# A hybrid decoder layer on one core: the output projection by seven half products for eight in blocks 7 to 14

## What is computed

```python
h = rmsnorm(x, norm_g)
proj = h @ w_in
q_g, k_g, v_g, gk_lr, gate_g, u_p, gate_p, q_m, gate_m = jnp.split(proj, SPLIT_IDX, axis=-1)
...
gk = jax.nn.log_sigmoid(gk_logit) / GLA_NORMALIZER
o_gla = gla_chunked(...)                 # 4 heads, chunks of 64, a carried state
o_gla = (rmsnorm(o_gla, gla_norm_g).reshape(B, T, D_GLA) * silu(gate_g))
o_pool = (pooled @ pool_w * pool_scale * silu(gate_p))   # windows 2, 4, 8, 16
o_mem = (softmax(q_m k_m) v_m) * silu(gate_m)            # 256 memory rows
mixed = jnp.concatenate([o_gla, o_pool, o_mem], axis=-1)
x = x + mixed @ w_out
return rmsnorm(x, final_g)
```

## Time and profile before

| | |
|---|---|
| median of three runs | 1374.71 us (1374.44 to 1376.68) |
| the profiled execution | 1374.43 us, span 1372.7 us |
| PE, PEld busy | 98%, 74% |
| DVE, ACT, POOL busy | 62%, 57%, 27% |
| DMA | 269.33 MB, mean 196 GB/s |
| chain that ended last | PE 94%, DVE 3%, ACT 1%, DMA 1% |
| L682 (values and output projection), L721 (seven-product groups), L700 (whole groups) | 34%, 33%, 10% of the chain |

### The profile page before, as it was taken

The page is one execution under the profiler, slowest core; times in us unless marked ns, Lnnn a source line. Parts: engine busy times, 40 slices in busy tenths (PEclk is TensorE's granted clock), DMA queues, the critical chain, the costliest instruction groups (busy, mean ns, idle before and its releaser), DMA issues.

```text
span 1372.7 us, 35629 instructions
## 1 busy us (share of the span) xinstructions
PE 1348.0 (98%) x14751; PEld 1012.2 (74%) x14751; DVE 844.3 (62%) x1598; ACT 783.9 (57%) x1446; POOL 371.6 (27%) x313
## 2 busy tenths in 40 slices
PE   6999999999999999999999999999999999999997
PEld 5788668586695968769586785958779596876953
DVE  6876667576555565565665655566565556566455
ACT  7896645555545565564646546464664556556353
POOL 2120163135322142332223223222332214233100
PEclk9999999999999999999999999999999999999999
DMA  9576657663663737466374754637466373745641
GB/s 385 192 214 210 215 181 236 194 245 121 215 247 94 285 100 264 182 184 245 94 293 124 242 205 149 251 96 278 150 215 247 111 270 98 264 181 183 241 101 47
DMA packets 143768, 269.33 MB, mean 196 GB/s; under 512 B 75152, under 2 KB 88720, under 8 KB 140432
## 3 DMA queue, kind: packets, MB, share of 16 engines
q1 hardware_dynamic: 142912, 266.20, 56.8%
q10 hardware_dynamic: 720, 1.06, 0.2%
HBM read 220.03 MB, written 30.41 MB: 182 GB/s over the span
## 4 chain that ended last, share of the span: by engine, by line
PE 94%; DVE 3%; ACT 1%; DMA 1%; issue 1%; SPq 0%; ACTq 0%; DVEq 0%
PE bank L682 34%; PE bank L721 33%; PE bank L700 10%; PE bank L916 2%; PE bank L942 2%; PE bank L936 2%; PE bank L1002 2%; PE bank L927 1%; PE bank L1032 1%; PE bank L957 1%; PE bank L803 1%; PE bank L900 1%; DVE arena L1638 1%; DMA out_parts<-fg 1%; PE bank L787 1%
## 5 line engine op out<-in xcount | busy, mean ns | idle before, releaser
L682 PE MATMUL bank<-ring,arena 128*128 128x512 f16 x1440 | 318.6, 379 | 0.0
L682 PEld LDWEIGHTS bank<-ring,arena 128*128 128x128 f16 x1440 | 138.5, 98 | 165.3 <-issue 5.9
L721 PE MATMUL bank<-arena,ring 128*128 128x128 f16 x4032 | 237.1, 219 | 0.0
L721 PE MATMUL bank<-arena,wres 128*128 128x128 f16 x4032 | 237.0, 219 | 0.0
L721 PEld LDWEIGHTS bank<-arena,ring 128*128 128x128 f16 x4032 | 228.4, 98 | 5.2 <-DVE arena L1616 1.8
L721 PEld LDWEIGHTS bank<-arena,wres 128*128 128x128 f16 x4032 | 227.7, 98 | 2.5 <-issue 2.5
L682 PE MATMUL bank<-wv,arena 128*128 128x512 f16 x768 | 168.5, 379 | 0.2 <-DVE wv L1602 0.2
L2136 POOL TENSOR_TENSOR arena<-arena 128x1024 f32<-128x1024 f32 (+2 forms) x42 | 64.8, 1543 | 352.9 <-ACT arena L1082 350.7
L682 PEld LDWEIGHTS bank<-wv,arena 128*128 128x128 f16 x768 | 75.0, 98 | 87.8 <-DVE wv L1602 0.4
L2144 POOL TENSOR_TENSOR arena<-arena 128x1024 f16<-128x1024 f32 x32 | 67.5, 2130 | 194.9 <-ACT arena L1100 182.3
L700 PE MATMUL bank<-arena,wres 128*128 128x256 f16 x768 | 86.1, 273 | 0.4 <-DVE wres L1580 0.4
(11 more groups left out here) (268 smaller groups left out, 2085.2 us busy)
## 6 DMA issues: line engine op xcount, KB each, us to landing
ring<-out_parts SPq DMA_DIRECT2D x120, 512.0 KB, 5.4
ring<-gate_parts SPq DMA_DIRECT2D x92, 512.0 KB, 5.8
ring<-side_parts SPq DMA_DIRECT2D x92, 512.0 KB, 6.3
arena<-in_xt SPq DMA_DIRECT2D x16, 1024.0 KB, 6.0
arena<-in_x SPq DMA_DIRECT2D x32, 512.0 KB, 4.4
out<-arena SPq DMA_DIRECT2D x31, 512.0 KB, 2.9
arena<-in_w_out SPq DMA_DIRECT2D x16, 512.0 KB, 5.3
out_parts<-arena SPq DMA_DIRECT2D x6, 512.0 KB, 6.4
```

What stands on the lines that cost most here:

```text
L682: mm = nc.tensor.matmul(ap, lhs, rhs, start=k == 0 and n == 0, stop=(k, n) == last)
L721: mm = nc.tensor.matmul(ap, w[:, p, k, j * P:(j + 1) * P], x_part(r, b)[:, k, :], start=fresh and j == 0 and k == 0 and n == 0, stop=k == ...
```

## The change

- **Products.** In steps 7 to 14 (of blocks 6 to 13's rows) the output product is a 2x2 block product over rows, features and columns with seven half products of 12 matmuls (`out_seven`). They stand where the quarters stood: 0 and 1 for quarter 0, 2 and 3 for 1, 4 and 5 for 2, and 6 alone for 3. They go to banks 0, 1, 0, 1, 6, 0, 1; products 2 and 5 add onto what stands in bank 0. Products 0 to 3 and 6 use rows of `mixed` (in the second half of the rows the two feature halves have been summed in place), product 2 the sum S2, products 4 and 5 a second set of sums written over the first rows of `mhl`.
- **Sums of mixed rows** (`mixed_sums`, POOL): three tensor_tensor, of 512, 512 and 1024 elements, at the start of step i, once the maximum of mixed is known; the third writes into `yb`'s place and waits for its store. ACT and DVE split them (`split_hi`, `split_lo`, two each per block).
- **Additions.** `add_seven` on DVE, nine of 512 elements in place of four. The first 128 rows of y have a place of their own (`y0`).
- **Sums of W_out.** In blocks 3 to 6 a pair of tiles of W_out is loaded per block (`pair_in`), scaled (`pair_scaled`, ACT), summed (`out_sums`, four tensor_tensor of 512 elements on POOL), split (`sums_hi`, `sums_lo`) and stored to DRAM (`sums_out`, 1 MB). ACT's x_plain moves behind norm_y there, and behind p_hi(3) in steps 7 to 14.
- **Loads.** 14 slots of 512 KB per block for the output product in place of 8; those for products 4, 5 and 6 are issued between the turns (the DMA transposes of the memory probabilities), before the loads of the next block's gates.
- **Blocks 4 to 6** are written out; the loop is over 7 to 14.

```diff
@@ -86,6 +86,11 @@
...
+OUT_BANK = (0, 1, 0, 1, 6, 0, 1)
+OUT_SLOT = ((7, 2), (3, 4), (5, 6), (0, 1), (2, 7), (3, 4), (5, 6))
+OUT_SPLIT = (1, 1, 2, 1, 3, 3, 1)
...
@@ -199,6 +229,10 @@
...
+        y0 = view(O_TP + 4096, [D], F32)
+        s43 = view(O_Y, [KT, P], F32)
+        wpair = [view(O_TP + 4096 * n, [2, 512], F32) for n in range(2)]
+        wsum = view(O_MIX, [4, 2, 512], F16)
...
@@ -372,7 +407,9 @@
...
-            with eng.Fori(WHOLE, NB - 1) as i:
+            for i in range(WHOLE, SEVEN):
+                step(i, False, False, False)
+            with eng.Fori(SEVEN, NB - 1) as i:
                 step(i, False, False, False)
...
@@ -431,6 +477,38 @@
...
+            def pair_in(i):
+                k = sum_row(i)
+                if is_whole(i):
+                    sp.wait_ge(lo_c, COMBINED + len(MADE))
+                else:
+                    sp.wait_ge(ad[PM], 4 * (i + 1))
+                    sp.wait_ge(q_ok, 2 * (i + 1))
+                    sp.wait_ge(qm_lo, 2 * (i + 1))
+                for n in range(2):
+                    sp.dma_start(wpair[n].rearrange("p h c -> p (h c)"), w_out[:, k + 4 * n, :]).then_inc(d_wot[n], 16)
+            def sums_out(i):
+                k = sum_row(i)
+                sp.wait_ge(lo_o, KT + 2 * k + 2)
+                sp.dma_start(sums_d[:, :, k // 2, :, k % 2, :], wsum).then_inc(d_wot[2], 16)
...
@@ -497,10 +575,23 @@
...
+            def residual_seven(i, t):
+                j = i - 1
...
+                else:
+                    sp.wait_ge(m_lo, mixed_split(i) + 3)
+                sp.dma_start((y0, yb)[t], x[j * TB + t * P:j * TB + (t + 1) * P, :]).then_inc(d_res, 16)
...
@@ -561,6 +652,50 @@
...
+                    to_slot(7, wo_d[:, 0, 0, :, :, :].rearrange("p r k c -> p (r k c)"))
+                    sums_in(3, T1)
+                    sp.wait_ge(pe_f[PM], 3 * i + 2)
+                    to_slot(2, wo_d[:, 0, 1, :, :, :].rearrange("p r k c -> p (r k c)"))
+                    quads_in(1, 0, 1)
+                    sp.wait_ge(pe_f[PM], 3 * i + 3)
+                    sum_in(2, T2, 0)
+                    residual_seven(i, 0)
+                    turn(i, 0)
+                    turn(i, 1)
+                    sp.wait_ge(pe_out, out_made(i) + 1)
+                    quads_in(4, 1, 1)
+                    sp.wait_ge(pe_out, out_made(i) + 2)
+                    sums_in(5, T3)
+                    residual_seven(i, 1)
+                    turn(i, 2)
+                    turn(i, 3)
+                    sp.wait_ge(pe_out, out_made(i) + 3)
+                    sums_in(6, T4)
+                    sp.wait_ge(pe_out, out_made(i) + 4)
+                    gates_in((0, 1))
+                    sp.wait_ge(pe_out, out_made(i) + 5)
+                    gates_in((2,))
+                    sides_in((0,))
+                    sp.wait_ge(pe_out, out_made(i) + 6)
+                    gates_in((3, 4))
+                    store(i - 1, 0)
+                    sp.wait_ge(pe_out, out_made(i) + 7)
+                    gates_in((5, 6))
+                    sp.wait_ge(d_store, 16 * (2 * i - 1))
...
@@ -575,22 +710,26 @@
...
+                    if makes_sums(i):
+                        pair_in(i)
                 for n in range(4):
                     turn(i, n)
+                if makes_sums(i):
+                    sums_out(i)
...
@@ -748,16 +887,38 @@
...
 
+            def out_seven(i, n):
+                pe.wait_ge(m_hi, mixed_split(i) + OUT_SPLIT[n])
+                pe.wait_ge(m_lo, mixed_split(i) + OUT_SPLIT[n])
+                if n in (2, 3, 5):
+                    pe.wait_ge(y_add, rows_added(i) + {2: 1, 3: 2, 5: 3}[n])
+                if n == 4:
+                    pe.wait_ge(sT_ok, 2 * i + 2)
+                if n == 6:
+                    pe.wait_ge(y_add, rows_added(i) + 8)
+                for s in OUT_SLOT[n]:
+                    pe.wait_ge(d_slot[s], 16 * loads("out" if n < 4 else "more", i, s))
+                first, t = 4 * (n in (1, 5, 6)), n in (3, 6)
+                for k in range(4):
+                    w = ring[:, OUT_SLOT[n][k // 2], :].rearrange("p (r k c) -> p r k c", r=2, k=2)
+                    for m, (p, r) in enumerate(((0, 0), (0, 1), (1, 0))):
+                        lhs = s2hl[:, p, k, :] if n == 2 else mhl[:, p, first + k, t * P:(t + 1) * P]
+                        mm = nc.tensor.matmul(bank[OUT_BANK[n]][:, :], lhs, w[:, r, k % 2, :],
+                                              start=n not in (2, 5) and k == 0 and m == 0, stop=k == 3 and m == 2,
+                                              skip_group_check=True)
+                mm.then_inc(pe_out, 1)
             def mix_sum(n):
 
...
@@ -953,12 +1114,17 @@
...
                 def quarter(n):
-                    if not first:
+                    if is_seven(i, last):
+                        for m in ((0, 1), (2, 3), (4, 5), (6,))[n]:
+                            out_seven(i, m)
...
@@ -1202,17 +1368,44 @@
...
+            def split_hi(i, n):
+                if n == 2:
+                    act.wait_ge(ms_ok, 3 * (i - SEVEN) + 2)
+                    nc.scalar.activation(s2hl[:, 0, :, :], sg[0], ACT.Copy, scale=s_m).then_inc(m_hi, 1)
+                else:
+                    act.wait_ge(ms_ok, 3 * (i - SEVEN) + 3)
+                    act.wait_ge(pe_out, out_made(i) + 2)
+                    nc.scalar.activation(mhl[:, 0, :, 0:P], s43, ACT.Copy, scale=s_m).then_inc(m_hi, 1)
...
@@ -1382,6 +1582,8 @@
...
+                    if is_seven(i, last):
+                        split_hi(i, 2)
...
@@ -1449,6 +1651,10 @@
...
+                elif makes_sums(i):
+                    pair_scaled(i)
+                elif is_seven(i, last):
+                    split_hi(i, 3)
...
@@ -1460,8 +1666,15 @@
...
-                if not first:
-                    norm_y(i - 1, 0)
+                if is_seven(i, last):
+                    x_plain(i + 1)
+                    norm_y(i - 1, 0, rows_added(i) + 5, y0)
+                elif not first:
+                    if makes_sums(i):
+                        sums_hi(i)
+                    norm_y(i - 1, 0, rows_added(i) + 2)
+                if makes_sums(i):
...
@@ -1695,9 +1908,23 @@
...
+            def sums_lo(i, n):
+                k = sum_row(i)
+                dve.wait_ge(hi_o, KT + 4 * k + 3 + n)
+                nc.vector.tensor_tensor(wsum[:, 2 * n:2 * n + 2, 1, :], wpair[n], wsum[:, 2 * n:2 * n + 2, 0, :],
+                                        ALU.subtract).then_inc(lo_o, 1)
+            def split_lo(i, n):
+                dve.wait_ge(m_hi, mixed_split(i) + n)
+                out2 = (s2hl[:, 0, :, :], s2hl[:, 1, :, :]) if n == 2 else (mhl[:, 0, :, 0:P], mhl[:, 1, :, 0:P])
+                nc.vector.scalar_tensor_tensor(out2[1], sg[0] if n == 2 else s43, s_m, out2[0], ALU.mult,
+                                               ALU.subtract).then_inc(m_lo, 1)
...
@@ -1707,18 +1934,33 @@
...
+            def add_seven(i, m):
+                t, h, b, made, before = (None, (0, 0, 0, 1, 0), (0, 0, 1, 2, 1), (0, 1, 0, 3, 0), (0, 1, 1, 4, 3),
+                                         (0, 1, 6, 5, 4), (1, 0, 0, 6, 0), (1, 1, 0, 6, 0), (1, 1, 1, 4, 7),
+                                         (1, 0, 1, 7, 6))[m]
+                if m in (1, 6):
+                    dve.wait_ge(d_res, 16 * (2 * i - 1 + t))
+                if m == 1:
+                    dve.wait_ge(sc_ok, i)
+                dve.wait_ge(pe_out, out_made(i) + made)
+                if before:
+                    dve.wait_ge(y_add, rows_added(i) + before)
+                row = (y0, yb)[t][:, h * 512:h * 512 + 512]
+                nc.vector.scalar_tensor_tensor(row, bank[b][:, :], sc_out, row, ALU.mult, ALU.add).then_inc(y_add, 1)
...
@@ -1884,6 +2128,8 @@
...
+                    if is_seven(i, last):
+                        split_lo(i, 2)
...
@@ -1999,9 +2245,15 @@
...
-                rows(0)
+                if is_seven(i, last):
+                    add_seven(i, 1)
+                else:
+                    rows(0)
                 mem_max(2)
                 mem_max(3)
+                if is_seven(i, last):
+                    split_lo(i, 3)
+                    add_seven(i, 2)
...
@@ -2010,11 +2262,21 @@
...
-                rows(1)
+                if is_seven(i, last):
+                    add_seven(i, 3)
+                else:
+                    rows(1)
...
                 state(3)
-                if not first:
-                    norm_rows(i - 1, 0)
+                if makes_sums(i):
+                    sums_lo(i, 0)
+                    sums_lo(i, 1)
+                if is_seven(i, last):
+                    for m in (4, 5, 6, 7, 8):
+                        add_seven(i, m)
+                    norm_rows(i - 1, 0, rows_added(i) + 5, y0)
+                elif not first:
+                    norm_rows(i - 1, 0, rows_added(i) + 2)
...
@@ -2031,13 +2293,15 @@
...
+                if makes_sums(i):
```

(30 more changed lines are left out.)

159 lines of the change are left out of this document (119 added, 40 removed).

## The result

The changed kernel takes **1414.33 us** (median of 4 runs, 1411.95 to 1417.72) against 1374.68 for the kernel before in the same job: ratio 1.0283, 95% interval 1.0269 to 1.0297. So it is slower by 39.7 us. The forecast was slower by 15.9 us, 1390.3, and its range ended at 1401: the direction was right, the size was not.

A forecast was written before the change was run, and what follows sets the result against it. TensorE, busy 98% of the span, was taken as the bound. Blocks 7 to 14 at +1.5 us each gave +12.0, blocks 4 to 6 +3.9; +15.9 on 1374.4 made 1390.3 us, range 1367 to 1401.

The forecast's parts named there:

- Twelve matmuls fewer, -2.6: Output product, blocks 7 to 14: seven products of 12 matmuls replace four quarters of 24, saving 2.6 us per block.
- Waits for a bank, +1.4: Output product, blocks 7 to 14: products 2 and 3 wait for adds 1 and 2 to free banks, +1.4 us per block.
- Waits for a slot, +0.4: Output product, blocks 7 to 14: product 4's loads, issued behind two transposes, land late, +0.4 us per block.
- The third sum stops the scans, +1.8: Ahead of GG phase 1, blocks 7 to 14: GpSimd's 1024-element sum blocks VectorE's softplus step or scans, +1.8 us per block.
- End of a block, +0.5: Blocks 7 to 14: GpSimd's x_end falls on VectorE's head multiplications, ahead of QK phase 0, +0.5 us per block (0 to 1.5).
- Blocks 3 to 6, +1.3 each for three, 0 for the first: Making sums of W_out delays y's store, residual load and rows(2): +1.3 us in blocks 4, 5 and 6, nothing in 3.
- the first (the sums don't stop the scans): Rival, blocks 7 to 14: scans run unhindered and x_end costs nothing, -0.8 us per block, 1370.4 us in all; chance 0.27.
- The second (slots decide): Rival, blocks 7 to 14: products 4, 5 or 6 wait 1 us more per block for loads, 1398 us; chance 0.10.
- The third: Rival: the port costs about half, or bank waits are only 0.75; near 0 per block, 1376 us; chance 0.15.

The follow-up runs named there:

- late_adds: late_sums with, in blocks 7 to 14, add 1 moved ahead of the first p_low and add 2 ahead of the second: 1396.20 us, ratio 1.0151.
- late_sums: The changed kernel with GpSimd's three sums of mixed rows held until VectorE's scans of the same step are over: 1391.93 us, ratio 1.0123.
- third_late: The changed kernel with only GpSimd's third sum of mixed rows (1024 elements) held until the scans are done: 1391.05 us, ratio 1.0115.
- before_one_sum: The kernel before the change plus one unused 1024-element GpSimd difference, released as the scans start, in blocks 4 to 14: 1388.76 us, ratio 1.0092.
- filled_gap: The changed kernel with seven unused matmuls put into TensorE's idle time ahead of GG phase 1 in blocks 7 to 14: 1407.67 us, ratio 1.0236.
- store_first: The changed kernel with, in blocks 3 to 6, the norm and store of y ahead of the sums of W_out: 1405.83 us, ratio 1.0211.
- residual_first: late_adds with product 4's loads ahead of the transposes and store_first's order, plus the residual load ahead of the 1 MB of sums: 1368.10 us, ratio 0.9951.
- residual_split: residual_first with, in blocks 3 to 6, ScalarE's first split of xb moved behind the last softmax half, ahead of the norm: 1378.98 us, ratio 1.0038.
- all_four: late_adds with product 4's loads ahead of the transposes, store_first's order, and the xb split back behind the scaled pair: 1382.23 us, ratio 1.0054.

## Why the prediction was right and where it was wrong

By its own steps:

- *Twelve matmuls fewer, -2.6.* Right: 2.60.
- *Waits for a bank, +1.4.* Right, with mechanism and size: 0.97 ahead of product 2 and 0.45 ahead of product 3 (I had 0.75 and 0.6). The late_adds run shows that on their own they were no loss, as the slots stood right behind them.
- *Waits for a slot, +0.4.* Right: 0.46 ahead of product 4.
- *The third sum stops the scans, +1.8.* Right: 1.87 in the trace. Held back it gives the time back (late_sums, third_late), and by itself it costs it in the kernel before (before_one_sum). By the Trainium skill's rule that the prediction cited ("SBUF — State Buffer", section "Who interferes with whom") the scans had to be stopped; these rows agree.
- *End of a block, +0.5.* 0.7: 0.33 ahead of QK phase 0 and 0.37 from there to GG phase 0, where the lrs copy is late. The head multiplication reads 1.35 us in place of 0.68, as GpSimd's x_end now falls on it.

These add up to about +1.9 where I had +1.5, and the intervals without a fall of the clock say the same (83.3 against 81.47). Without the clock, blocks 7 to 14 lost 19.1 - 6.7 = 12.4 us, and the prediction said 12.0. That these two are so near is in part luck: seven intervals lose 1.9 each, not eight 1.5, and the last, from block 14 to 15, has no third sum ahead of it and wins 0.4.

Two things were wrong:

- *The missing term.* The prediction gave every wait its length and stopped there ("each wait put in front of TensorE costs its full length"). Behind an idle time of 1.74 us the next phase ran for part of its length with 0.50 of the clock granted. It cost 6.7 us in steps 8 to 12, shown by filled_gap, and by the lengths of three phases (5.81, 6.78, 5.81 in place of 4.18) 5.9 us in blocks 4 to 6, together 12.6 of the 39.7. That the clock falls behind the idle time and is kept up when the idle time is filled was shown for blocks 7 to 14; in blocks 4 to 6 it is read from the trace. The Trainium skill ("TensorE: Matmul & The Clock Gate", section "HAM oscillation — how this bites in real kernels") tells of a kernel in which TensorE waits for a DMA in every tile and starts the next one at the lower clock each time. The waits there are longer than those here; the trace shows that 1.74 us was enough, but only in four of seven steps. I had drawn on the skill for the port alone.
- *Blocks 3 to 6, +1.3 each for three, 0 for the first.* The step named the right chain (sums, then store, then residual load, then rows(3)) and had its price too low: "2 us for the engine, some 2 for the queue". (Its own times, 938.9 against 937.4, give 1.5 and not 1.3.) VectorE was held back not only by its two new instructions (2.35 us) but also in norm_rows, by 1.9 us, since GpSimd's split of xb had been pushed behind the sums too. The queue cost no more than I had given it: 4.4 us from the store's issue to the load's, where a store landed after 2.9 before. In block 4 rows(2) starts 42.5 us behind the values product, where it started 36.8 behind it in block 10 before: 5.7 us later and not 4. I had worked out the port's price with care for blocks 7 to 14 and had left it here to a bracket, "the upper end with contention". Idle time ahead of QK phase 0 was 1.3, 3.7, 3.7 and 2.3 us, 11.0 in all, against 3.9. That block 3 pays nothing was wrong too: it pays the first of these, 1.3. With the 5.9 us of clock this is 16.9 of the 17.6 us that these blocks lost.

The rivals: the first (the sums don't stop the scans) is refuted. Nor does its size hold where the scans are let go: it put -0.8 on a block, and late_sums shows 0.0, since the end of a block keeps its 0.7. That its 1370.4 us is near the time of the kernels with the other waits taken out too (1371.85 and 1368.10) is chance. The second (slots decide) was wrong for the change as it stands and became true as soon as the banks were cleared, in late_adds. The third was not it.

What stays open: why the clock fell in steps 8, 10, 11 and 12 and not in 9, 13 and 14, behind equal idle time. In store_first, whose steps from 7 on are the same program, it fell in steps 8, 9, 12 and 13, and in residual_first it did not fall in block 4 behind 1.94 us; so the step and the length of the wait alone do not decide it. The runs show that filling the idle time prevents it, and no more. And the rest of blocks 3 to 6 in the fastest kernel (5.6 us over the time before) was not taken out: two attempts to move the split of xb made it worse.

## What to carry to other kernels

An engine that is idle for most of the span is not free: ask for each instruction put on GpSimd which two-input instruction of VectorE runs at that moment, and whether TensorE waits for it; one semaphore wait that shifts it can be worth more than the saving for which it was added. When TensorE's input comes late, add to the wait what the clock loses behind it, and take waits out together: here banks alone cost 4 us, banks and slots won 15. And an order that frees y, its store and the next load comes before work that nobody waits for.

## What the hardware showed that I had not expected

Idle time of 1.7 to 3.7 us on TensorE was followed by 0.50 of the granted clock for part of the next phase in seven of the ten phases that follow such a wait in the changed kernel (three in blocks 4 to 6, four in steps 8 to 14), at a price of 1.6 to 2.6 us each; behind 0.8 to 1.0 us it was not, in eleven steps of before_one_sum. And what one pair of GpSimd subtractions of 1024 elements costs VectorE depends on what it meets there, short instructions or long: norm_rows with the two osq subtractions behind it lost 3.6 us in block 4 of the changed kernel (3.16 + 3.21 us, where 1.28 + 1.48 stand in residual_split), four p_low, 1.68 us together in block 10 of the changed kernel, lost 3.3 in all_four (5.01 us), and the osq subtractions alone lost 2.4 in store_first, where VectorE was idle for 1.23 us while the pair ran. Moving the pair, as all_four and residual_split did, took the loss off osq and put it on p_low, and both kernels got slower.
